# Token scales moved from the turned activations to the evictions of the first layer's projections, with the loads reordered

## What is computed

```
def rmsnorm(x, g):
    y = xf * lax.rsqrt(jnp.mean(xf * xf, axis=-1, keepdims=True) + RMS_EPS)
    return y * g
hn = rmsnorm(h, norm_mix[0])
proj = hn @ w_in
q, k, v, r, glr = jnp.split(proj, ...)          # 512, 512, 1024, 1024, 16 columns
glog = log_sigmoid(glr @ w_gate_up + b_gate) / 16
cum = cumsum(glog)                              # in chunks of 64 tokens
a = (q * exp(cum - mid)) @ (k * exp(mid - cum)).T
o = rmsnorm(masked a @ v + (q * exp(cum)) @ state, g_norm) * silu(r)
h = h + o @ w_out
```

## Time and profile before

| | us |
|---|---|
| median of 3 runs | 1584.37 |
| lowest and highest | 1582.99, 1586.37 |
| the profiled execution's time | 1583.33 |
| its span, first to last instruction | 1581.4 |
| PE, DVE, ACT, POOL busy | 1346.1, 972.3, 537.5, 564.5 |
| granted TensorE clock, mean | 0.966 |

### The profile page before, as it was taken

One profiled execution on the slowest core, in us unless ns is written; L12 is line 12 of the kernel. 1 busy time (PEld: TensorE's weight loads), 2 busy tenths in 40 slices (PEclk: granted clock), 3 DMA queues, 4 the chain that ended last, 5 costly groups with the idle time before them and its releaser, 6 DMA issues.

```text
span 1581.4 us, 14465 instructions
## 1 busy us (share of the span) xinstructions
PE 1346.1 (85%) x4096; PEld 664.7 (42%) x4096; DVE 972.3 (61%) x2428; ACT 537.5 (34%) x1638; POOL 564.5 (36%) x532
## 2 busy tenths in 40 slices
PE   7999899889776997889998699788899877777776
PEld 5555565445332443333555244333365432222222
DVE  3327598988774434763477856574557887554544
ACT  2324332323233223562323323564322323332322
POOL 1001345454442332444443333344444343333330
PEclk9999999999997999989999899999999999999998
DMA  9317999999999999999999999999999999999995
GB/s 380 145 53 293 377 408 421 421 421 420 421 421 422 421 420 422 419 402 410 421 421 420 422 420 421 421 405 396 422 421 420 421 421 421 423 421 422 421 422 212
DMA packets 85086, 620.39 MB, mean 392 GB/s; under 512 B 10352, under 2 KB 10352, under 8 KB 11280
## 3 DMA queue, kind: packets, MB, share of 16 engines
q0 software_dynamic: 74768, 551.65, 84.4%
q1 hardware_dynamic: 9792, 67.77, 10.4%
q10 hardware_dynamic: 448, 0.05, 0.0%
HBM read 618.38 MB, written 1.05 MB: 392 GB/s over the span
## 4 chain that ended last, share of the span: by engine, by line
PE 41%; DMA 39%; DVE 10%; ACT 7%; issue 3%; SPq 0%; POOL 0%; ACTq 0%; DVEq 0%; POOLq 0%
DMA arena<-in_peer_uv_dram,hnT 28%; PE banks L542 25%; PE banks L567 5%; PE banks L422 5%; DMA raw<-in_peer_uv_dram,hnT 5%; DMA work<-in_peer_uv_dram,hnT 4%; DVE arena L1422 3%; PE banks L688 2%; DMA rt<-in_diff_lambda_k_dram 2%; ACT g_e L930 2%; ACT hnT L919 1%; PE banks L514 1%; DVE raw L1422 1%; DVE work L1422 1%; ACT hnT L914 1%
## 5 line engine op out<-in xcount | busy, mean ns | idle before, releaser
L542 PE MATMUL banks<-arena,g_e 128*128 128x512 f32 x1184 | 575.5, 619 | 129.7 <-ACT g_e L930 128.7
L348 POOL DMA_INDIRECT arena<-in_peer_uv_dram,hnT x299 | 324.8, 1086 | 508.2 <-PE banks L542 498.4
L542 PEld LDWEIGHTS banks<-arena,g_e 128*128 128x128 f32 x1184 | 217.8, 196 | 404.8 <-issue 213.0
L1422 DVE CUSTOM_DVE_ANT_0 arena<-arena,hrows 128x1024 f32<-128x1024 f32 x209 | 253.9, 1222 | 153.9 <-DMA arena<-in_peer_uv_dram,hnT 149.8
L914 ACT ACTIVATE hnT<-hnT 128x2 f32<-128x2 f32 (+1 forms) x240 | 48.7, 203 | 697.0 <-DVE hnT L1422 692.2
L542 PE MATMUL banks<-raw,g_e 128*128 128x512 f32 x424 | 208.2, 622 | 41.3 <-ACT g_e L930 37.3
L348 POOL DMA_INDIRECT raw<-in_peer_uv_dram,hnT x106 | 115.8, 1092 | 178.2 <-PE banks L542 175.8
L930 ACT ACTIVATE g_e<-ident,hnT 128x128 f32<-128x128 f32 x501 | 172.7, 393 | 1.7 <-ACT hnT L919 0.6
L1422 DVE CUSTOM_DVE_ANT_0 arena<-arena,banks 128x1024 f32<-128x1024 f32 x90 | 109.6, 1220 | 85.4 <-DMA arena<-in_peer_uv_dram,hnT 85.3
L542 PEld LDWEIGHTS banks<-raw,g_e 128*128 128x128 f32 x424 | 78.3, 197 | 135.1 <-issue 78.4
L1422 DVE CUSTOM_DVE_ANT_0 raw<-raw,hrows 128x1024 f32<-128x1024 f32 x80 | 97.6, 1225 | 56.3 <-DMA raw<-in_peer_uv_dram,hnT 55.9
(11 more groups left out here) (236 smaller groups left out, 1299.5 us busy)
## 6 DMA issues: line engine op xcount, KB each, us to landing
arena<-in_diff_in_dram SPq DMA_DIRECT2D x24, 1024.0 KB
arena<-in_peer_query_dram SPq DMA_DIRECT2D x16, 1024.0 KB
arena<-in_gla_in_dram POOLq DMA_DIRECT2D x5, 2048.0 KB, 21.1
arena<-in_peer_query_dram SPq DMA_DIRECT2D x4, 2048.0 KB, 10.3
arena<-in_diff_out_dram SPq DMA_DIRECT2D x8, 1024.0 KB
arena<-in_peer_uv_dram,hnT POOLq DMA_INDIRECT x299
work<-in_gla_out_dram POOLq DMA_DIRECT2D x2, 2048.0 KB, 40.1
arena<-in_gla_in_dram SPq DMA_DIRECT2D x2, 1024.0 KB, 12.2
```

What stands on the lines that cost most here:

```text
L348: pool.indirect_dma_start(pair(n), None, table, bass.IndirectOffsetOnAxis(ap=places[:, o:o + 1].bitcast(u32), axis=0)).then_inc(S(f"pair_l ...
L542: last = nc.tensor.matmul(bank(2 * (tile % NT) + half), diags[:, slot * P:(slot + 1) * P], v_row(n)[:, half * 512:(half + 1) * 512], start ...
L1422: V.tensor_tensor_reduce(out=u_row(n), in0=u_row(n), in1=normed, scale=1.0, scalar=0.0, op0=ALU.mult, op1=ALU.add, accum_out=dots[:, o:o + ...
```

## The change

The token scale no longer goes on the turned activations. `hnT` gets the gain alone, four of its eight steps on ACT and four on DVE, as soon as it and the gains are there. `scale_rows` moves from the start of PE's program into q1, after its first half, and into bank 2; ACT copies its result to `arena` (`A_SPREAD`). The evictions then carry the scale: those of q, k and of the gate's 16 rows, where tokens lie along the row, move from ACT to DVE and multiply by the spread scales (`turned_out`, `gate_low_out`), those of v and r, where a token is a partition, stay on ACT and take the scale as a per-partition factor. `gate` moves from q0 to k0, `gla_scores` from before v1 to after it, and the orders of ACT and DVE change with them. SP issues the turned activations first, then block 0, then the rows; POOL waits for `x1_loaded` in place of `xt_loaded`.

```
+A_SPREAD = A_HX + (NT + 1) * P
 sync:
-            for m in range(NT):
-                sp.dma_start(h[:, m, :], x[0, m * P:(m + 1) * P, :]).then_inc(S(f"x{m}_loaded"), 16)
             sp.dma_start(hnT[:].rearrange("p m k t -> p (m k t)"), x_t).then_inc(S("xt_loaded"), 16)
             for half, loaded in ((0, "win_top_loaded"), (1, "win_bottom_loaded")):
...
+            for m in range(NT):
+                sp.dma_start(h[:, m, :], x[0, m * P:(m + 1) * P, :]).then_inc(S(f"x{m}_loaded"), 16)
 gpsimd:
-            pool.wait_ge(S("xt_loaded"), 16)
+            pool.wait_ge(S("x1_loaded"), 16)
 tensor:
-                    last = nc.tensor.matmul(bank(7)[:, m * P:(m + 1) * P], ar(A_HX + NT * P, P), ar(A_HX + m * P, P),
+                    last = nc.tensor.matmul(bank(2)[:, m * P:(m + 1) * P], ar(A_HX + NT * P, P), ar(A_HX + m * P, P),
...
-                    pe.wait_ge(S("hnT_ready"), k + 1)
+                    pe.wait_ge(S(("hnT_act", "hnT_dve")[k // 2 % 2]), k // 4 * 2 + k % 2 + 1)
...
-            scale_rows()
             gate_inner()
-            turned_heads("q", 0, gate)
-            turned_heads("q", 1)
-            turned_heads("k", 0)
+            turned_heads("q", 0)
+            turned_heads("q", 1, scale_rows)
+            turned_heads("k", 0, gate)
             turned_heads("k", 1)
             rows("v", 0)
+            rows("v", 1)
             gla_scores()
-            rows("v", 1)
 scalar:
                 act.preload_act_table(ACT.Sqrt)
+                act.wait_ge(sl, 16 * 2)
+                act.wait_ge(S("xt_loaded"), 16)
+                for k in (0, 1, 4, 5):
+                    A(hnT[:, :, k, :], hnT[:, :, k, :], ACT.Copy, scale=gains[:, G_MIX + k:G_MIX + k + 1]
+                      ).then_inc(S("hnT_act"), 1)
                 act.wait_ge(S("x0_loaded"), 16)
...
+                act.wait_ge(S("scale_spread"), 1)
+                A(ar(A_SPREAD, SEQ), bank(2)[:, 0:SEQ], ACT.Copy).then_inc(S("spread_ready"), 1)
...
-                unit_out("v", n, ar(A_V + n * 512, 512))
+                unit_out("v", n, ar(A_V + n * 512, 512), scale=row_scale(n))
...
             hx_rows()
-            gate_low_out()
-            sincos()
             gla_abs()
             gla_exp()
+            gla_ln()
+            sincos()
             lam_exps()
-            q_out(0)
-            gla_ln()
-            q_out(1)
             gla_exps()
-            k_out(0)
-            k_out(1)
             v_out(0)
+            v_out(1)
             gla_keys()
-            v_out(1)
 vector:
+                for k in (2, 3, 6, 7):
+                    V.tensor_scalar(hnT[:, :, k, :], hnT[:, :, k, :], gains[:, G_MIX + k:G_MIX + k + 1], None, ALU.mult
+                                    ).then_inc(S("hnT_dve"), 1)
...
+            def turned_out(kind, n):
+
+                dst = {"q": A_Q, "k": A_K}[kind] + n * 512
+                dve.wait_ge(S(f"{kind}_done"), n + 1)
+                spread = ar(A_SPREAD, SEQ).unsqueeze(1).broadcast_to([P, 2, SEQ])
+                V.scalar_tensor_tensor(out=ar(dst, 512).rearrange("p (j t) -> p j t", j=2),
+                                       in0=bank(unit_bank(kind, n)).rearrange("p (j t) -> p j t", j=2),
+                                       scalar=GDK ** -0.5 if kind == "q" else 1.0, in1=spread,
+                                       op0=ALU.mult, op1=ALU.mult).then_inc(S(f"{kind}_out"), 1)
...
             gla_ones()
             hx_rows()
-            hx_turned()
+            gate_low_out()
+            turned_out("q", 0)
+            turned_out("q", 1)
+            gla_z()
+            turned_out("k", 0)
             angles()
+            turned_out("k", 1)
             reduced(0)
             reduced(1)
-            gla_z()
             lam_dots()
             gla_scan()
```

More of the change, by code:

```diff
@@ L198, in trunk_kernel @@
         G_MIX, G_GLA, G_DIFF, G_BG = 0, 16, 24, 32
-        ST_SS, ST_V, ST_Y, ST_T, ST_DEC = 0, 8, 16, 24, 32
+        ST_SS, ST_V, ST_Y, ST_T, ST_DEC, ST_X = 0, 8, 16, 24, 32, 30
         words = hnT[:].rearrange("p m k t -> p (m k t)")
@@ L794, in unit_out, with row_scale @@
                 A(dst, bank(unit_bank(kind, n)), function, scale=scale).then_inc(S(f"{kind}_out"), 1)
[L796 to L800, removed]
+            def row_scale(n):
+                return stat[:, ST_X + n // 2:ST_X + n // 2 + 1]
             def v_out(n):
-                unit_out("v", n, ar(A_V + n * 512, 512))
+                if n == 0:
+                    act.wait_ge(S("row_scales"), 1)
+                unit_out("v", n, ar(A_V + n * 512, 512), scale=row_scale(n))
             def r_out(n):
-                unit_out("r", n, ar(A_R + n * 512, 512), ACT.Silu)
+                unit_out("r", n, ar(A_R + n * 512, 512), ACT.Silu, scale=row_scale(n))
             def query_out(n):
@@ L1132, in hx_rows @@
                 link(V.memset(ar(A_HX + NT * P, P), 1.0))
+                dve.wait_ge(S("small_loaded"), 16 * 2)
+                dve.wait_ge(S("xt_loaded"), 16)
+                for k in (2, 3, 6, 7):
+                    V.tensor_scalar(hnT[:, :, k, :], hnT[:, :, k, :], gains[:, G_MIX + k:G_MIX + k + 1], None, ALU.mult
+                                    ).then_inc(S("hnT_dve"), 1)
                 dve.wait_ge(S("x1_loaded"), 16)
@@ L1142, in hx_rows, with gate_low_out @@
                                     ).then_inc(S("scale_diags"), 1)
[L1144 to L1152, removed]
+                V.tensor_copy(stat[:, ST_X:ST_X + NT], stat[:, ST_Y:ST_Y + NT]).then_inc(S("row_scales"), 1)
+            def gate_low_out():
+                dve.wait_ge(S("spread_ready"), 1)
+                dve.wait_ge(S("gate_inner_done"), 1)
+                V.tensor_tensor(gate_low, bank(4)[0:GRANK, 0:SEQ], arena[0:GRANK, A_SPREAD:A_SPREAD + SEQ], ALU.mult
+                                ).then_inc(S("gate_low_ready"), 1)
+            def turned_out(kind, n):
[6 more added lines that the diff above has]
+                                       op0=ALU.mult, op1=ALU.mult).then_inc(S(f"{kind}_out"), 1)
             def chunked(ap):
```

## The result

The changed kernel took 1586.07 us (median of 22 runs, 1582.79 to 1588.74) against 1583.74 us (22 runs, 1581.61 to 1589.21) for the kernel before in the same sessions. The ratio is 1.0015 with a 95% interval of 1.0009 to 1.0020: slower by 2.4 us, between 1.4 and 3.2, which is less than the 0.2% that the prediction called no change. The profiled execution of it has a span of 1583.7 us against 1581.4.

A forecast was written before the change was run, and what follows sets the result against it. PE was taken as the bound between 60 and 162 us, passing early shifts through to the end. Early units -0.1 plus clock 1.7 gave +1.6 us: 1584.9 profiled, 1586.0 for the median; range 1582.2 to 1588.8.

The forecast's parts named there:

- The start of PE: Start of gate_inner, before the turned heads: released by w_glr at 8.1 us in place of 11.39.
- Rival 5: Start of PE: gate_inner no sooner, at 11 as before; 1588.9 us; chance 0.16 together with rival 2.
- The cold gate_inner: PE's first unit: still 5.7 us at the lower clock (4.8 to 6.6), so q0 starts at 13.8.
- rival 4: Start of PE: warm after all, clock column taken literally, q0 at 11.5; 1582.0 to 1583.7 us; chance 0.06.
- q0 to k1: PE from q0's start to k1's end: 30.3 us with scale_rows, no wait on a load, ending at 44.1.
- The chain: DVE and ACT work behind K, the end of k1: klT_ready for gla_scores at K + 17.9; PE pauses 4.2 us.
- Rival 3: Before gla_scores: no pause, as DVE has the range reductions done by then; -4.3 us, 1580.1; chance 0.04.
- The pause of the kernel before: PE before gla_scores in the kernel before: 1.30 us, taken as fixed, with the set of early units ending at 65.03.
- The clock's fall: PE's granted clock falls to 0.50 in or behind the pause before gla_scores: 1.7 us lost, 0 to 3.0.
- Rival 1: Pause before gla_scores: clock holds or little is lost; -1.0 to +0.8 us, around 1584.3; chance 0.19.
- rival 2: Late w_glr or gains, long slow spell: +4.8 us, 1589.2; decides once q0's start plus clock loss passes 17.1; 0.16 with Rival 5.
- The sum: Whole kernel: -0.1 us at PE's early units plus 1.7 us of clock, +1.6 us; r0 near 66.6; chance 0.55.

The follow-up runs named there:

- warm start: Changed kernel with 14 idle matmuls on PE ahead of gate_inner: 1584.38 us, ratio 1.0001 to the kernel before.
- early reductions: Changed kernel with DVE running angles, both range reductions and lam_dots before gla_z, not behind k1: 1579.86 us, ratio 0.9974 to the kernel before.

## Why the prediction was right, and where it was off

- **What bounds the kernel.** Held. Whatever moved r0 moved the first gather by as much, over a spread of 16 us.
- **The start of PE.** w_glr was the releaser at 8.19, 8.1 forecast. The gain went on from 6.89, 0.7 us later than the 6.2 that I took: it was released by the gate's up projection, which shares a semaphore with the gains, and those had landed at 6.2 (5.4 us after their issue at 0.82). ACT's last step was done at 8.6 in place of 7.8. Neither held PE: it started on w_glr, and came to the later steps when they were done. Rival 5, no earlier start at all, fell.
- **The cold gate_inner.** It moved with the start as forecast. The size was one value, 5.7 us, with 4.8 to 6.6 as ends; starts between 8.14 and 8.24 gave 4.97, 5.22, 5.49, 5.94 and 6.41 (8.19 to 8.24 for the lowest and the highest), mean 5.6. That q0's mean over the two traces of the changed kernel, 13.8, is the forecast figure is luck: 5.7 was one draw too. The first trace alone would have looked like a success of an early start. Reading the clock column literally (rival 4) was wrong: the idle work in front shows what a warm gate_inner takes, 3.63 us, while the column reads 1.00 in cold and warm alike. The rule that was set against it, in the Trainium skill's page "TensorE: Matmul & The Clock Gate", Part 1 (an idle array starts at 1.2 GHz and gets 2.4 GHz only after sustained work), agrees with these traces: 0.43 us between weight loads at first, about 0.21 later.
- **q0 to k1.** 30.3 us forecast, 30.30 measured (43.39 less 13.09). Block 1 landed 9.3 us after its issue at 14.99, at 24.3, and PE came to k0 at 27.5.
- **The chain.** K + 17.9 forecast, 17.81 measured; the pause 4.2 forecast, 3.92 measured, and 3.90 to 3.92 in five traces of kernels with that chain. Its steps are work of DVE and ACT with no load among them, and it doesn't scatter. Rival 3 fell.
- **The pause of the kernel before.** This is the term that was mis-sized. The sum took its 1.30 us as the kernel's and compared 64.9 with 65.03. It belonged to one execution: the lambda loads landed at 38.49 there and at 37.45 in the second trace, where there was no pause and v1 began 1.04 us sooner (56.96 for 58.00). With that trace for the kernel before the same sum gives +0.9 in place of -0.1. The row named its releaser, the load, and a load that shares its way with 14 MB of weights should have been given a range.
- **The clock's fall.** It came, as in the nine pauses. The price taken was 1.7 us, one end of what the rows showed; the first trace had 1.7, the second 2.9, and in the warm start it was 0.50 over all of 6.0 us, 3.0 us. Both values had stood in the earlier trace rows, and the long one was given less weight than it had. Rival 1, the clock holds, fell. The condition of rival 2 was met in one of the two traces, though by another way than a late load: 14.58 + 2.9 = 17.5, above its 17.1.
- **The sum.** +1.6 forecast, +2.4 (1.4 to 3.2) measured. By the mean of two traces each, r0 moved from 64.4 to 66.7, +2.3. The error of 0.8 us is these two terms, the pause of the kernel before and the clock's price, each read off single executions; q0 was 3.5 us sooner on the mean, for 3.3 forecast. The forecast r0, 66.6, lies between the 65.51 and 67.86 of the two traces, so neither of them alone could have confirmed or refuted it.

Still open is how often each low spell and each landing occurs, and why; two traces of each kernel show that they vary and not how.

## What to carry to other kernels

An earlier start is worth only what is left of it where engines next meet: here a chain of 18 us on two other engines hung on the last of PE's early units, with 4.0 us of independent work queued in it (eviction to scan 4.6 us, 0.6 without it) while its engine had just stood idle for 5. Price a pause of some 4 us on PE with the clock's fall behind it, 1.7 to 3 us. And count a pause, a landing or the clock's rise that one trace shows as one draw; take a second trace before you build a difference of 1 us on it.

## What was not expected

- A load of 64 KB (rows of 512 B) landed 6.4 us after its issue on POOL's queue and 8.8 and 8.0 us after it on ACT's, behind the gains, with the same large loads under way; and issued 0.44 us sooner on POOL's queue it landed at 8.14 in place of 8.19.
- The lambda loads, four of 32 KB, landed at 38.49 and 37.45 when they stood behind weights with POOL's blocks beside them, and by 18.9 (last issue at 4.96, at most 13.9 us) when POOL's blocks were issued behind them. The forecast had taken 36, at which DVE would have had to wait with the early reductions; there lam_dots ran at 31.95 and waited for nothing.
- The clock's low spell behind the same pause of 3.9 us costs 1.7 us in one execution and 2.9 in another of the same kernel.
